# A hybrid transformer layer on one core: its last normalisation split over three engines, and its first input in another order

## The reference

```python
(a_q, a_ckv, i_q, i_k, i_w, m_q, m_k, m_v, m_o, m_i, m_f, g_a, g_m) = _split_cols(h @ w_in[l])
kv = rms_norm(a_ckv, kv_norm[l]) @ w_ukv[l]
y_a = dsa_attention(a_q..., kv, i_q..., i_k, i_w)
y_m = mlstm(m_q..., m_k..., m_v..., m_i + m_i_bias[l], m_f + m_f_bias[l])
y_m = (y_m * jax.nn.sigmoid(m_o.astype(F32))).astype(h.dtype)
mix = jax.nn.sigmoid(g_a) * (y_a @ w_proj_a[l]) + jax.nn.sigmoid(g_m) * (y_m @ w_proj_m[l])
h = layer_norm(DN_ALPHA * h + mix @ w_out[l], ln1_g[l], ln1_b[l])
ff = hier_moe(h, w_grp[l], b_grp[l], w_exp[l], b_exp[l], w_gate[l], w_up[l], w_down[l])
ple = (p[l] @ w_ple[l]) * jax.nn.sigmoid(h @ w_ple_gate[l])
h = layer_norm(DN_ALPHA * h + ff + ple, ln2_g[l], ln2_b[l])
```

## Time and profile before

| | us |
|---|---|
| median of 3 runs (lowest, highest) | 1522.07 (1521.82, 1523.80) |
| the profiled execution's own time | 1522.69 |
| its span, first to last instruction | 1520.9 |
| busy in the span: PE, DVE, ACT, POOL | 1478.9, 687.0, 499.0, 53.8 |
| read from HBM, written | 391.71 MB, 2.10 MB |

### The profile page before, as it was taken

How to read it: one execution, slowest core, us unless ns; L and a number is a source line. 1 busy time by engine, 2 the same in 40 slices (tenths; PEclk the granted TensorE clock), 3 DMA queues, 4 the chain that set the end, 5 groups by cost and what they waited for, 6 DMA issues and landing times.

```text
span 1520.9 us, 16838 instructions
## 1 busy us (share of the span) xinstructions
PE 1478.9 (97%) x6636; PEld 996.3 (66%) x6636; DVE 687.0 (45%) x952; ACT 499.0 (33%) x674; POOL 53.8 (4%) x62
## 2 busy tenths in 40 slices
PE   8999999999999999999999999999999999999893
PEld 7887788888877888888888887534434443353331
DVE  5546665457646555454445655431212312221126
ACT  4444444455544443444444433411100200020011
POOL 0000000043300000000000000000000000000000
PEclk9999999999999999999999999999999999999997
DMA  8654555554443556555565876499999999999994
GB/s 305 197 175 157 166 171 193 189 166 140 140 154 121 173 172 204 194 192 189 196 193 182 321 259 225 161 407 421 391 406 416 371 417 413 419 381 418 420 405 163
DMA packets 132733, 394.89 MB, mean 260 GB/s; under 512 B 13232, under 2 KB 15920, under 8 KB 108080
## 3 DMA queue, kind: packets, MB, share of 16 engines
q1 hardware_dynamic: 124080, 386.56, 68.7%
q10 hardware_dynamic: 8576, 7.28, 1.4%
HBM read 391.71 MB, written 2.10 MB: 259 GB/s over the span
## 4 chain that ended last, share of the span: by engine, by line
PE 61%; issue 37%; DVE 1%; DMA 0%; ACT 0%; POOL 0%; POOLq 0%; DVEq 0%; SPq 0%
PE bank L498 19%; PE bank L499 19%; PE bank L503 19%; PE bank L525 1%; PE bank L678 1%; PE bank L700 1%; PE bank L612 1%; DMA x_rows<-in_x_dram 0%; PE bank L691 0%; PE bank L727 0%; PE bank L726 0%; DVE res L2247 0%; DVE res L2253 0%; PE bank L785 0%; PE bank L737 0%
## 5 line engine op out<-in xcount | busy, mean ns | idle before, releaser
L1560 DVE TENSOR_TENSOR w_lo<-w_ring,w_hi 128x1024 fp32r<-128x1024 f32 (+1 forms) x312 | 381.9, 1226 | 305.4 <-ACT w_hi L1134 304.2
L1134 ACT ACTIVATE w_hi<-w_ring 128x1024 fp32r<-128x1024 f32 (+1 forms) x312 | 327.4, 1051 | 310.7 <-PE bank L503 308.2
L498 PE MATMUL bank<-w_hi,xT_hi 128*128 128x512 f32 (+1 forms) x864 | 346.7, 401 | 1.6 <-DVE xT_lo L1598 1.6
L499 PE MATMUL bank<-w_hi,xT_lo 128*128 128x512 f32 (+1 forms) x864 | 334.9, 388 | 0.0
L948 PE MATMUL bank<-moe_ring,xg 128*64 128x512 f32 x1024 | 226.3, 594 | 5.4 <-DMA moe_ring<-in_w_up_dram 3.3
L503 PE MATMUL bank<-w_lo,xT_hi 128*128 128x512 f32 (+1 forms) x864 | 229.3, 387 | 0.0
L498 PEld LDWEIGHTS bank<-w_hi,xT_hi 128*128 128x128 f32 x864 | 162.4, 188 | 37.8 <-issue 4.6
L499 PEld LDWEIGHTS bank<-w_hi,xT_lo 128*128 128x128 f32 x864 | 162.5, 188 | 32.2 <-issue 1.9
L503 PEld LDWEIGHTS bank<-w_lo,xT_hi 128*128 128x128 f32 x864 | 161.6, 188 | 33.2
L948 PEld LDWEIGHTS bank<-moe_ring,xg 128*64 128x64 f32 x1024 | 72.8, 137 | 153.0 <-issue 152.6
L884 PE MATMUL bank<-moe_ring,h1T 128*128 128x512 f32 x240 | 105.8, 594 | 0.0
(11 more groups left out here) (271 smaller groups left out, 1286.7 us busy)
## 6 DMA issues: line engine op xcount, KB each, us to landing
w_ring<-in_w_in_dram SPq DMA_DIRECT2D x103, 1024.0 KB, 5.0
moe_ring<-in_w_gate_dram SPq DMA_DIRECT2D x64, 1024.0 KB, 9.9
moe_ring<-in_w_up_dram SPq DMA_DIRECT2D x64, 1024.0 KB, 11.3
moe_ring<-in_w_down_dram SPq DMA_DIRECT2D x64, 1024.0 KB, 11.0
w_ring<-in_w_proj_a_dram SPq DMA_DIRECT2D x16, 1024.0 KB, 5.0
w_ring<-in_w_proj_m_dram SPq DMA_DIRECT2D x16, 1024.0 KB, 5.0
w_ring<-in_w_out_dram SPq DMA_DIRECT2D x16, 1024.0 KB, 5.1
moe_ring<-in_w_ple_gate_dram SPq DMA_DIRECT2D x15, 1024.0 KB, 9.7
```

Of the source, the lines that this page charges most:

```text
L498: mm(b, lh(k, m), WH[:, s, kk, 0:width], start=start and kk == 0, stop=False)
L499: mm(b, ll(k, m), WH[:, s, kk, 0:width], start=False, stop=False)
L1134: fn(WH[:, h % 4, :, 0:width], W32[:, h // 2, 2 * (h % 2):2 * (h % 2) + 2, 0:width], ACT.Copy).then_inc(hi_ready, 1)
L1560: v.tensor_tensor(WL[:, h % 4, :, 0:width], W32[:, h // 2, 2 * (h % 2):2 * (h % 2) + 2, 0:width], WH[:, h % 4, :, 0:width].bitcast(F32), A ...
```

## The change

- **Input.** SP issues columns 0 of x before the first weight half. ScalarE and VectorE split x's first columns ahead of the first weight half, not behind it. 20 turns of the identity for 24.
- **Maxima.** The product in `head_scores` runs over all 128 rows; GpSimd fills `negG` with zeros once.
- **Last pair.** `down_last(3)` runs in one piece, with `scatter(7, 2, 4)` behind it. VectorE takes the low part of part 3 between the third and fourth BN_STATS.
- **Arms.** On TensorE, ScalarE and VectorE the usual path stands in the first arm, `If(over < 1)`, and the overflow in `Else`; both end with the normalisation. VectorE's last two additions stand inside the arms. SP is as before.
- **Normalisation.** Block by block: aggregation, + eps on VectorE, the power on GpSimd. VectorE makes (x - mean) * gain for all eight parts in one operation each. Two parts (block 1, columns 2 and 3) it also finishes, * rstd + bias. For the other six, TensorE adds in one bank each the bias (a column of ones by the bias rows) and a diagonal matrix of rstd by the gained part; ScalarE makes the diagonal and copies the banks back to `RES`.

```diff
@@ constants @@
-PARTS = 8
+PE_PARTS = ((0, 0), (0, 1), (0, 2), (0, 3), (1, 0), (1, 1))
+DVE_PARTS = ((1, 2), (1, 3))
+NORM_ORDER = (("gain", 0, 0), ("gain", 0, 1), ("gain", 0, 2), ("gain", 1, 2), ("gain", 0, 3), ("gain", 1, 0), ("end", 1, 2),
+              ("gain", 1, 1), ("gain", 1, 3), ("end", 1, 3))
+GAIN_AT = {(a, c): i for i, (a, c) in enumerate(o[1:] for o in NORM_ORDER if o[0] == "gain")}
+OUT_ORDER = (("pe", 0), ("pe", 1), ("pe", 2), ("dve", 0), ("pe", 3), ("pe", 4), ("dve", 1), ("pe", 5))
@@ sync @@
+            x_columns(0)
             sp.dma_start(W32[:, 0, 0:2, :], first_rows(0, 2)).then_inc(first_in, 16)
-            x_columns(0)
             sp.dma_start(W32[:, 0, 2:4, :], first_rows(2, 2)).then_inc(landed[0], 16)
...
-            for k in range(PARTS):
-                a, c = k // 4, k % 4
-                sp.wait_ge(nrm_done, k + 1)
+            for who, k in OUT_ORDER:
+                if who == "pe":
+                    sp.wait_ge(n2_out, k + 1)
+                else:
+                    sp.wait_ge(nrm_done, k + 1)
+                a, c = (PE_PARTS if who == "pe" else DVE_PARTS)[k]
@@ gpsimd @@
+            link(g.memset(negG[:], 0.0))
...
-            deviation(2)
+            for a in range(NT):
+                pl.wait_ge(var_ready, 2 + a)
+                g.tensor_tensor(rstd[:, a:a + 1], rstd[:, a:a + 1], mhalf[:, 0:1], ALU.pow).then_inc(rstd_ready, 1)
@@ tensor @@
-            for n in range(24):
+            for n in range(20):
...
-                mm(B[4][:, 0:TOK], ident[0:MH, h:h + 1].to_broadcast([MH, P]), negG[0:MH, :], start=True, stop=True)
+                mm(B[4][:, 0:TOK], ident[:, h:h + 1].to_broadcast([P, P]), negG[:], start=True, stop=True)
...
-            down_last(3, lambda k: scatter(7, 2, 4) if k == 2 else None)
+            down_last(3)
+            scatter(7, 2, 4)
             scatter(7, 3, 6)
...
-            with pe.If(over > 0):
+            def second_norm():
+
+                pe.wait_ge(ln2_in, 32)
+                for j, (a, c) in enumerate(PE_PARTS):
+                    if j == 4:
+                        pe.wait_ge(y_add, 2 * SCATTER_AT[7, 2] + 2)
+                    mm(B[j][:, :], ident[:, 0:1].to_broadcast([P, P]), ln2b[:, c * NC:c * NC + NC], start=True, stop=False)
+                for j, (a, c) in enumerate(PE_PARTS):
+                    pe.wait_ge(n2_diag, a + 1)
+                    pe.wait_ge(nrm_g, GAIN_AT[a, c] + 1)
+                    mm(B[j][:, :], dg[:, a, :], RES[:, a, c * NC:c * NC + NC], start=False, stop=True).then_inc(n2_mm, 1)
+
+            with pe.If(over < 1):
+                second_norm()
+            with pe.Else():
@@ scalar @@
-                if h == 1:
-                    x_turned(0)
-                if h and h % 2 == 0:
+                if h % 2 == 0:
                     x_turned(h // 2)
...
+            def rows_normed():
+
+                for a in range(NT):
+                    ac.wait_ge(rstd_ready, 2 + a)
+                    fn(dg[:, a, :], ident[:], ACT.Identity, scale=rstd[:, a:a + 1]).then_inc(n2_diag, 1)
+                for j, (a, c) in enumerate(PE_PARTS):
+                    ac.wait_ge(n2_mm, j + 1)
+                    fn(RES[:, a, c * NC:c * NC + NC], B[j][:, :], ACT.Copy).then_inc(n2_out, 1)
+
+            with ac.If(over < 1):
+                rows_normed()
+            with ac.Else():
@@ vector (x_turned as on scalar) @@
-            statistics(1, link)
+            statistics(1, link, (0,))
+            y_part(7, 3)
+            statistics(1, link, (1,))
             add(7, 2, 4)
             dv.wait_ge(y_add, 2 * SCATTER_AT[7, 2] + 2)
             statistics(2, link)
-            y_part(7, 3)
...
+                for step, a, c in NORM_ORDER:
+                    s = slice(c * NC, c * NC + NC)
+                    if step == "gain":
+                        stt(out=RES[:, a, s], in0=RES[:, a, s], scalar=mv2[:, 2 * a:2 * a + 1], in1=ln2g[:, s], op0=ALU.subtract,
+                            op1=ALU.mult).then_inc(nrm_g, 1)
+                    else:
+                        dv.wait_ge(rstd_ready, 2 + a)
+                        dv.wait_ge(nrm_g, GAIN_AT[a, c] + 1)
+                        stt(out=RES[:, a, s], in0=RES[:, a, s], scalar=rstd[:, a:a + 1], in1=ln2b[:, s], op0=ALU.mult,
+                            op1=ALU.add).then_inc(nrm_done, 1)
+
+            with dv.If(over < 1):
+                for a in range(NT):
+                    last_add(a)
+                    statistics(3, link, (a,))
+                    last_moments(a, link)
+                second_norm()
+            with dv.Else():
```

More of the change, by code:

```diff
@@ L224, in build @@
         negG = at("neg_running_max", [TOK], ZC + 3072)
+        dg = at("rstd_diagonal", [NT, P], ZC + 2048)
         small = at("small", [768], ZS)
@@ L282, in build @@
         h1_hi, h1_lo, res_gain, res_ready = sem("h1_hi"), sem("h1_lo"), sem("res_gain"), sem("res_ready")
-        nmr_ready = sem("nmr_ready")
         ple_in, pT_mm, pT_c, pp_mm, pp_c = sem("ple_in"), sem("pT_mm"), sem("pT_copied"), sem("pp_mm"), sem("pp_copied")
@@ L1519, in _ @@
                         y_part(n, c)
-            with ac.If(over > 0):
+            def rows_normed():
[8 more added lines that the diff above has]
+            with ac.Else():
                 ac.wait_ge(y_mm, 2 * CHUNKS * NP)
@@ L1538, in _ @@
                                 fn(ygh[:, c, :], B[4 + c][:, :], ACT.Copy).then_inc(o_yh, 1)
-            ac.wait_ge(nmr_ready, 1)
-            for k in range(PARTS):
-                a, c = k // 4, slice(k % 4 * NC, k % 4 * NC + NC)
-                fn(RES[:, a, c], RES[:, a, c], ACT.Identity, bias=nmr[:, a:a + 1], scale=rstd[:, a:a + 1]).then_inc(nrm_a, 1)
+                rows_normed()
         @block.vector
@@ L1933, in _, with moments @@
             mean, var = (mv2.rearrange("p (a n) -> p a n", n=2)[:, :, k] for k in range(2))
-            def moments(n):
+            def moments(n, link):
                 for a in range(NT):
@@ L1956, in residual @@
                 v.tensor_tensor(RES[:, a, :], RES[:, a, :], lnb[:], ALU.add).then_inc(res_ready, 1)
-            moments(1)
+            moments(1, link)
             for a in range(NT):
@@ L2195, in _, with last_add, last_moments, second_norm @@
             statistics(2, link)
-            y_part(7, 3)
-            for a in range(NT):
+            def last_add(a):
                 add(7, 3, 6, (a,))
                 dv.wait_ge(y_add, 2 * SCATTER_AT[7, 3] + a + 1)
-                statistics(3, link, (a,))
-            with dv.If(over > 0):
+            def last_moments(a, link):
+                link(v.bn_aggr(mv2[:, 2 * a:2 * a + 2], bnst[:, 24 * a:24 * a + 24]))
+                v.tensor_scalar(rstd[:, a:a + 1], mv2[:, 2 * a + 1:2 * a + 2], EPS, None, ALU.add).then_inc(var_ready, 1)
+            def second_norm():
+                dv.wait_ge(ln2_in, 32)
+                for step, a, c in NORM_ORDER:
[13 more added lines that the diff above has]
+                    last_moments(a, link)
+                second_norm()
+            with dv.Else():
                 link2 = Link(dv, dve_over)
+                for a in range(NT):
+                    last_add(a)
                 for r in range(3):
@@ L2234, in _ @@
                     statistics(c, link2)
-            moments(2)
-            stt(out=nmr, in0=mean, scalar=-1.0, in1=rstd, op0=ALU.mult, op1=ALU.mult).then_inc(nmr_ready, 1)
-            dv.wait_ge(ln2_in, 32)
-            def part(k):
-                a, c = k // 4, slice(k % 4 * NC, k % 4 * NC + NC)
-                return RES[:, a, c], c
-            def gained(k):
-                r, c = part(k)
-                dv.wait_ge(nrm_a, k + 1)
-                v.tensor_tensor(r, r, ln2g[:, c], ALU.mult).then_inc(nrm_g, 1)
-            def finished(k):
-                r, c = part(k)
-                dv.wait_ge(nrm_g, k + 1)
-                v.tensor_tensor(r, r, ln2b[:, c], ALU.add).then_inc(nrm_done, 1)
-            gained(0)
-            for k in range(1, PARTS):
-                gained(k)
-                finished(k - 1)
-            finished(PARTS - 1)
+                for a in range(NT):
+                    last_moments(a, link2)
+                second_norm()
 _INS = ['x', 'p', 'w_in', 'kv_norm', 'w_ukv', 'm_i_bias', 'm_f_bias', 'w_proj_a', 'w_proj_m', 'w_out', 'ln1_g', 'ln1_b',
```

3 lines of the change are left out of this document (2 added, 1 removed).

## The result

| | before | after |
|---|---|---|
| median of 4 runs, us (lowest, highest) | 1521.94 (1521.65, 1523.80) | 1512.18 (1511.48, 1512.62) |
| the profiled execution's own time | 1522.69 | 1512.39 |
| its span | 1520.9 | 1510.5 |

The ratio of after to before is 0.9931, with a 95% interval of 0.9918 to 0.9943; the medians are 9.8 us apart. The forecast was 1512.9. The ratio times the median of before gives 1511.4, just under the low end of the range (1511.5). The total is near, but it is near because two wrong terms of opposite sign stand in the sum. The rows show which. All ratios in this document are of fast runs; two slow runs of a_rows8, at 1889.95 and 4353.62 us with a granted clock of 0.75 and 0.34, stand in none.

A forecast was written before the change was run, and what follows sets the result against it. TensorE was taken as the bound (97% busy) except in the first 10 us and last 25 us, where VectorE's chain sets the end. Start 1.5 plus tail 7.7 saves 9.2 from median 1522.07: 1512.9, range 1511.5 to 1516.0.

The forecast's parts named there:

- Start: First 10 us: x first and 20 warm-ups bring the first product from 9.96 to near 8.4, saving 1.5 (1.1 to 1.8).
- the swap: Input transfers: x and the equally large weight half exchange landing times, x at 4.8 and the weight half at 7.2.
- Maxima: Product in the eight heads over 128 rows: 426 against 431 ns, 0.04 us at most, priced at nothing.
- Before the last additions: Tail, last down product in one piece and VectorE's reordered chain: last two additions start at 1499.3 instead of 1499.64, saving 0.3.
- The jump: Tail branch: VectorE's 3.15 us idle over the overflow code goes; jumps at the arms' ends cost 0.1 (0 to 0.5).
- second rival: Diagonal products in the tail run at TensorE's lower clock, last one ending 4.9 later: 1517.8; 10%, 8 with the bias-products case.
- first rival: Tail branch: the stall stays, its new arm not at hand or the 3.15 not the jump's: 1515.9, 10%.
- Normalisation: Tail: first gain 3.9 after the last additions start, ten operations at 0.6, ScalarE's last copy at 10.75, GpSimd's power hidden.
- T: Start of VectorE's first of the last two additions in the tail: 1499.64 before, forecast 1499.3, or near 1497.8 with the earlier start.
- Landing: End of the tail: output landing and end 2.82 as before, plus 0.2 (0 to 0.8) for eight outputs in 4.5 us.
- the clock held over the gap before the first product: Denied rival: first dense stretch at the lower clock after the shorter warm-up, 1563 if over the first 50 us; 3%.
- The third: Rival: the start gives nothing, because x lands at 7 anyway or the clock rises later: 1514.4, 9%.

The follow-up runs named there:

- a_rows8: The kernel after with the maxima product on 8 rows again instead of 128; span 1513.6 us, ratio to before 0.9959.
- a_arms_swapped: The kernel after with the overflow in the first arm and the usual path second on TensorE, ScalarE and VectorE; span 1514.1 us, ratio to before 0.9952.
- a_pe_second: The kernel after with TensorE's usual path as second arm and its bias products ahead of the branch; median 1511.48 us, ratio to before 0.9925.

## Why the prediction was right or wrong, point by point

- **Start, 1.5.** Right in its mechanism: first product forecast near 8.4, seen at 8.41. The transfer of x was 0.65 later than the swap said, and it cost nothing. As a size it was the luck of this profile: over ten kernels it is 0.4 to 1.5, near 1.0 (from leads, not from one paired measurement). I took the warm-ups at their mean of 0.195 each; they run 0.213 or 0.109 apart, by the clock, and when the clock rises decides how much of the saving is left.
- **Maxima, "Nothing", 0.04 at most.** This step failed, and it alone is nearly a third of the gain between the two profiles: 3.17, eight times 0.40. I compared two neighbouring rows of the trace of before, 426 and 431, and both carried the cost that I was looking for. I read the duration of a product and not the distance between starts, nor the idle time of the weight loads ahead of it.
- **Before the last additions, 0.3.** 0.13. TensorE's scatter no longer stands ahead of the additions, as said, and 0.21 stands at the branch.
- **The jump, 3.15.** Right, and shown both ways by the idle time (3.01 back, 0.04 left); over runs the size is less sure (above). The branch that is not taken costs 83 ns on TensorE and the one that is taken 3.3 to 4.9 us; where the prediction says that the 108 ns would lead to the second rival's time, it is the first rival's, 1515.9. The exit jumps, which I put at +0.1 as a question of ScalarE's time, did cost something, but elsewhere: ScalarE was out in 0.5 us, and the jumps brought code packets among the last outputs.
- **Normalisation.** Right, to 0.16: first gain at T + 3.65 (forecast 3.9), gains 0.66 apart, diagonal products at 1.00 clock, the last copy done at T + 10.91 (10.75). GpSimd's second power took 0.99 beside VectorE's gains and was hidden, as forecast. Its first reader is not the finishing step that the prediction names (2.8 us later), but ScalarE's second diagonal, which started 0.04 behind it at 1499.69 and was itself not needed before the fifth diagonal product. The prediction takes the operations at 0.68 in words and at 0.6 in the sum; they came 0.66 apart.
- **Landing, 0.2 (0 to 0.8) and the jump 0.1 (0 to 0.5).** This term failed too: from the last copy to the end 4.74, not 3.15, 1.6 more and over both bounds together. Of the 1.9 that the last landing took beyond the first, 0.4 to 1.1 is crowding and the rest code packets, which the prediction did not have.
- **The rivals.** The stall did not stay, TensorE's clock did not fall before its last product, and the clock held over the gap before the first product. The second one came true by half in a_arms_swapped: behind a stall the bias products ran at the lower clock, the diagonal ones did not, and it cost 0.1. The third names a later rise of the clock; that is what took 0.2 to 1.1 of the start's 1.5 in seven of the ten kernels.

So without the 3.17 of the maxima the forecast would have been 1.9 us too low: 0.2 at T, 0.16 in the normalisation and 1.59 behind it. 3.17 in the other direction hid that, and turned it into 1.2 too high on the spans (1511.7 forecast, 1510.5 measured). That the total came so near is luck.

## What to carry to other kernels

Before an edit is priced at nothing from two rows of a trace, look for a row that surely is free of its effect: a product over 128 rows far from any smaller one would have read 379 ns and not 431. Where a small product stands between full ones, fill the free rows with zeros and run over all 128. A jump is paid at the place where its engine has nothing queued: put it behind work that is already handed over (on TensorE it then cost nothing, in a_pe_second), and count the jump out of an arm as traffic that the last outputs will meet. Before a start is priced from one trace, look how far its pace differs between traces of the same start.

## What the runs showed of the hardware that I had not expected

- One product over 8, 32 or 64 rows between products over 128 costs 0.40 us, the same for all three.
- A jump out of an arm, 3.3 to 4.9 us on TensorE, comes with packets of 8 KB and 16 KB; with three or more of them among the outputs the last landing took 4.0 to 4.9 us, with none or a single one of 8 KB 2.1 to 3.4.
- TensorE's branch ran for 3.39 us while its queued products went on. The Trainium skill, Advanced Engine Details and Errata, section Engine Queue Depths, gives TensorE a queue of 64 and VectorE one of 8; in this trace nine of the twelve passes on TensorE start while its branch runs or after it.
- TensorE's clock rose to its full level between 4.43 and 7.63 us in thirteen kernels that begin with 20 or 24 transposes at 1.6 us, and at 14.38 us in the one with 8. Ahead of the rise the printed granted clock is 1.00 and means nothing; there the pace has to be read from the distance of starts (0.213 us for a transpose, 0.109 behind the rise). In the tail, where the list has entries, it is seen: 0.56 in before, 0.57 in a_arms_swapped.
- In the expert stage, where the DMA share is 0.99, the lead of a kernel over before moves by up to 1.3 us and partly back (after: 4.64 at 1040 us, 5.48 at 1150, 4.18 at 1350, 4.54 at 1480). Tails are better compared from T than by spans: the way from T to the last copy is 10.91 in nine of the ten profiles with the new tail, and 11.00 in a_arms_swapped.
